# Start-up of a two-layer mixer kernel: loads in one queue in order of need, 16 KB weight rows, means from ScalarE's square, the second group's norm ahead of the output projection

## What is computed

```
h = rmsnorm(x, norm_g)                        # x * rsqrt(mean(x*x) + 1e-6) * g
a_in, a_gate, u, v, b_gate = h @ w_in         # five blocks of 512 columns
a = pool_mix(a_in) * silu(a_gate)             # trailing means over 2/4/8/16 rows, w_pool, a scale
b = u * (tril(w_s) @ rmsnorm(v, per head) + b_s) * silu(b_gate)    # chunks of 128 rows
x = x + concat(a, b) @ w_out
```

## Time and profile before

| what | value |
|---|---|
| median of three runs | 496.17 us |
| the profiled execution: its time | 495.29 us |
| its span (first to last instruction, slowest core, core 3) | 493.7 us |
| spans of the eight cores | 489.3 to 493.7 us |
| TensorE busy | 461.2 us (93%) |
| VectorE, ScalarE, GpSimd busy | 328.8, 176.2, 102.1 us |
| granted TensorE clock, core 3 | 0.987 |

### The profile page before, as it was taken

The page is one execution under the profiler, slowest core; times in us unless marked ns, Lnnn a source line. Parts: engine busy times, 40 slices in busy tenths (PEclk is TensorE's granted clock), DMA queues, the critical chain, the costliest instruction groups (busy, mean ns, idle before and its releaser), DMA issues.

```text
span 493.7 us, 7731 instructions; the slowest of 8 cores (489.3 to 493.7 us)
## 1 busy us (share of the span) xinstructions
PE 461.2 (93%) x2428; PEld 214.1 (43%) x2428; DVE 328.8 (67%) x654; ACT 176.2 (36%) x294; POOL 102.1 (21%) x142
## 2 busy tenths in 40 slices
PE   3878979999899899999999999999999999999991
PEld 1423435444444345444544445444454445444440
DVE  3666636668965768767788658655774667885665
ACT  3223251392024612229224650014800381333144
POOL 8341010510034100161015200024000500161000
PEclk9989989999999999999999999999999999999997
DMA  7999999990029500450027000000000000220013
GB/s 195 155 159 161 207 197 201 167 138 8 1 59 156 85 1 1 172 172 2 1 90 253 4 3 1 0 1 28 4 1 0 1 1 1 85 93 19 1 42 128
DMA packets 22659, 36.97 MB, mean 75 GB/s; under 512 B 1822, under 2 KB 16670, under 8 KB 22588
## 3 DMA queue, kind: packets, MB, share of 16 engines
q0 software_dynamic: 14912, 14.94, 22.1%
q1 hardware_dynamic: 6844, 20.38, 13.3%
q10 hardware_dynamic: 864, 1.16, 0.7%
...
## 4 chain that ended last, share of the span: by engine, by line
PE 83%; DMA 6%; ACT 3%; DVE 3%; issue 2%; POOL 1%; another core or an unknown queue 0%; ACTq 0%; DVEq 0%; POOLq 0%
PE pF L514 55%; PE pF L1001 19%; DMA win<-w_in 6%; PE pT L498 3%; PE pF L974 2%; PE pF L738 1%; PE pF L937 1%; ACT vscr L776 1%; POOL win L310 1%; DVE xg L1007 1%; ACT vscr L473 1%; ACT hT L811 1%; PE pF L965 1%; DVE hT L502 0%
## 5 line engine op out<-in xcount | busy, mean ns | idle before, releaser
L514 PE MATMUL pF<-hT,win 128*128 128x512 bf16 x1024 | 233.0, 381 | 4.6 <-DVE vn_sb L607 3.0
L514 PEld LDWEIGHTS pF<-hT,win 128*128 128x128 bf16 x1024 | 99.1, 98 | 121.8 <-issue 9.5
L1001 PE MATMUL pF<-wout,mix 128*128 128x512 bf16 x512 | 116.8, 383 | 2.9 <-DMA wout<-w_out 2.5
L1001 PEld LDWEIGHTS pF<-wout,mix 128*128 128x128 bf16 x512 | 49.3, 99 | 61.1 <-issue 8.0
L597 POOL TENSOR_TENSOR ss<-ss,nhalf 128x4 f32<-128x4 f32 (+1 forms) x34 | 37.2, 1094 | 152.8 <-DVE ss L595 152.6
L514 PE MATMUL pF<-win,hT 128*128 128x512 bf16 x272 | 60.8, 379 | 1.1 <-DVE hT L502 1.1
L473 ACT ACTIVATE vscr<-xg 128x1024 bf16<-128x1024 f32 x40 | 42.2, 1056 | 45.7 <-DVE xg L1007 39.0
L1007 DVE TENSOR_TENSOR xg<-pF,xg 128x512 f32<-128x512 f32 x64 | 44.0, 688 | 21.7 <-PE pF L1001 20.1
L588 ACT ACTIVATE vscr<-pF 128x512 f32<-128x512 f32 x32 | 19.1, 597 | 98.1 <-PE pF L514 68.8
L488 ACT ACTIVATE hb<-xg,ssx 128x1024 bf16<-128x1024 f32 x28 | 32.0, 1143 | 59.0 <-PE pT L498 52.3
L482 POOL TENSOR_TENSOR ssx<-ssx,nhalf 128x1 f32<-128x1 f32 (+1 forms) x22 | 15.0, 681 | 181.1 <-DVE ssx L480 163.1
...
## 6 DMA issues: line engine op xcount, KB each, us to landing
...
```

What stands on the lines that cost most here:

```text
L514: r = h.matmul(out=out_ap, lhsT=lhsT(k), rhs=rhs(k), start=(k == 0), stop=(k == 7))
L1001: r = h.matmul(out=pf[:, :], lhsT=mix[:, k, i * 128:(i + 1) * 128], rhs=wout[l][:, k, hf * 512:(hf + 1) * 512], start=(k == 0), stop=(k == 7))
```

## The change

1. The first item's loads stand in GpSimd's queue, in this order: x tiles 1 to 3, v block, v_norm_g, a_in, a_gate, w_pool, b_gate, the first part of w_s, u, first half of w_out, x tiles 4 and 5, second half of w_out, x tiles 6 and 7. SP keeps x tile 0. None of them waits for a landing any more. `prep_ws(0)` moves behind the b_gate products.
2. Layer 1's weights are issued by GpSimd in item 1, after its v tiles (`load_second`).
3. w_in, w_out and v_norm_g are laid out anew in HBM on the host. A block of 512 columns is 128 partition rows of 16 KB in one piece, where it was 1024 rows of 2 KB; v_norm_g is there 128 times instead of being read 128 times.
4. The square's `scale` is D^-0.5 (for v 128^-0.5), so its sum is the mean. The VectorE instruction for mean plus epsilon goes; epsilon is added on GpSimd, ahead of the power. The last item keeps its way, without the factor.
5. `norm_first`: tiles 2 and 3 are scaled on ScalarE.
6. Item 0: squares and scalings of the second group's tiles 0 and 1 stand ahead of `out_mm`, the others behind its first half; the first two transposes stand ahead of `out_mm(1, 1)`.

```diff
-    win_d = din("w_in", [2, D, DIN])
+    win_d = din("win_h", [2, 5, 128, 4096])
-    wout_d = din("w_out", [2, D, D])
+    wout_d = din("wout_h", [2, 2, 128, 4096])
-        win = [sb(f"win{l}", [128, 8, DIN], BF16) for l in range(2)]
+        win = [sb(f"win{l}", [128, 5, 8, 512], BF16) for l in range(2)]
...
-        for t in range(4):
-            load_tile(t)
-        for cb in WIN_ORDER:
-            if cb == C_BGATE:
-                load_wpool(0)
-            load_win(0, cb)
-        load_wout(0)
-        for cb in WIN_ORDER:
-            load_win(1, cb)
-        load_wpool(1)
+        load_tile(0)
+        for t in range(1, 4):
+            load_tile(t, eng=POOL)
         ldma(g_bc[:, 0:258], bsr_d[:, :], buf("bsf"))
-        ldma(vg_bc[:, 0, :], bc(vng_d[0:1, :]), buf("vg_bc0"), deps=[wop[f"w0_{C_V}_2"]])
-        stage(stg[:, 0:640], wsk_d[:, 0:640], [buf("mask"), buf("wsf0")], deps=[wop[f"w0_{C_AIN}_0"]])
-        for t in (4, 5):
-            load_tile(t, deps=[wop[f"w0_{C_U}_0"]])
-        for t in (6, 7):
-            load_tile(t, deps=[wop["wout0_0"]])
+        load_win(0, C_V)
+        ldma(vg_bc[:, 0, :], vng_d[0], buf("vg_bc0"), eng=POOL)
+        load_win(0, C_AIN)
+        load_win(0, C_AGATE)
+        load_wpool(0)
+        load_win(0, C_BGATE)
+        stage(stg[:, 0:640], wsk_d[:, 0:640], [buf("mask"), buf("wsf0")], eng=POOL)
+        load_win(0, C_U)
+        load_wout(0, (0,))
+        load_tile(4, eng=POOL)
+        load_tile(5, eng=POOL)
+        load_wout(0, (1,))
+        load_tile(6, eng=POOL)
+        load_tile(7, eng=POOL)
         stage(stg[:, 640:1152], wsk_d[:, 640:1152], buf("wsf1"), deps=[wop["wout0_1"]])
...
+        def rstd_from(c, cb_, rb, nparts=128):
+            pool_rsqrt(rsx[0:nparts, c:c + 1], ssx[0:nparts, c:c + 1], nhalf[0:nparts, 0:1], [cb_], [rb])
+        def pool_rsqrt(out, ms, expo, rd, wr):
+            S.emit(POOL, lambda h: h.tensor_scalar(out=out, in0=ms, scalar1=EPS, scalar2=None, op0=ALU.add), reads=rd, writes=wr)
+            S.emit(POOL, lambda h: h.tensor_tensor(out=out, in0=out, in1=expo, op=ALU.pow), reads=wr + [buf("nhalf")],
+                   writes=wr)
...
+            else:
+                S.emit(ACT, lambda h: h.activation(out=hb[:, i % NHB, :], in_=xa, func=AF.Copy, scale=rsx[:, c:c + 1]),
+                       reads=[xbuf(0, i), rb], writes=[buf(f"hb{i % NHB}")])
...
-                hk["v"] = [lambda: prep_ws(0)]
+                hk["bg"] = [lambda: prep_ws(0)]
             if n == 1:
+                hk["v"] = [load_second]
...
+        def load_second():
+            for cb in WIN_ORDER:
+                load_win(1, cb)
+            load_wpool(1)
...
             if n == 0:
+                nrm.square(0)
+                nrm.square(1)
+                nrm.rstd(0, 2)
+                nrm.scale(0)
+                nrm.scale(1)
                 for i in range(TPG):
                     out_mm(i, 0)
-                    nrm.square(i)
-                    nrm.rstd(i, 1)
-                    if i < 3:
-                        nrm.scale(i)
+                nrm.square(2)
+                nrm.rstd(2, 1)
+                nrm.scale(2)
+                nrm.square(3)
+                nrm.rstd(3, 1)
                 out_mm(0, 1)
-                out_mm(1, 1)
                 norm_tr(*nx, 0)
                 nrm.scale(3)
                 norm_tr(*nx, 1)
+                out_mm(1, 1)
                 out_mm(2, 1)
```

94 lines of the change are left out of this document (44 added, 50 removed).

## The result

The changed kernel takes **489.77 us** (median of four runs, 489.29 to 489.98) where the kernel before takes 496.10: ratio 0.987, 95% interval 0.9853 to 0.9887. In some executions of every kernel one die ran at a lower clock and the time was longer; medians here count all runs, while ratios and mean spans leave those out. The profiled execution took 489.68 us with a span of 488.1 on core 4, so the spans differ by 5.6 us from the profile before.

A forecast was written before the change was run, and what follows sets the result against it. Before 82 us, weight landings, TensorE and waits for w_out and v's scaling were taken to bound the kernel. Terms -2.1 - 2.5 - 1.8 + 0.4 + 2.1 + 0.3 = -3.6 took 496.17 to 492.6 us, range 489.8 to 496.9.

The forecast's parts named there:

- a_gate's start: Item 0: a_gate's products begin at 35.7 us instead of 37.76, worth -2.1 us; wrong if not before 37.
- the instructions called off the path: VectorE's means: 59 instructions, some 9.6 us, go without touching the critical path.
- w_out's wait, -2.5: End of item 0: w_out's second half lands at 65.3, before TensorE comes at 66.9, so its wait goes.
- the clock behind it, -1.8: Behind the w_out wait: the lowered clock goes, 16 products taking 3.46 us instead of 5.30.
- Tile 7, +0.4: End of item 0: the last x tile's late norm delays TensorE 0.4 us, between no wait and 1 us.
- Item 1, +2.1: GpSimd's six weight issues take D = 3.9 us ahead of pooling; TensorE waits D - 1.8 at the bias product, 1.7 to 3.4.
- under 1 or over 4: Sign against the forecast: item 1's wait, put at about 2 us, lies outside 1 to 4 us.
- Item 2, +0.3: Norm chains lengthened by GpSimd's addition make TensorE wait 2.0 us instead of 1.7 in item 2; 0 to 0.6.
- Part 6 at no cost: End of item 0: second-group squares and scalings lie beside the first 32 output products, 6.9 us, and cost nothing.
- the first (the loads come no faster): Before item 1: loads keep their old rate, w_out lands at 68.0, only order gains; 496.0 us, chance 0.18.
- The second, GpSimd's issues: Item 1: the six issues make the kernel slower, deciding from D = 7.5; 499.2 us at D = 10.5, chance 0.12.
- The third, the larger gain: Loads at 330 GB/s, no lowered clock at 31 us, D = 3.5, a_gate at 34.7: 490.7 to 489.2 us, chance 0.12.

The follow-up runs named there:

- e15: The changed kernel with all four first-group x scalings on VectorE, as before the change, instead of two on ScalarE: 488.64 us.
- e2: The changed kernel with w_in and w_out read in short rows of 2 KB again: 493.21 us.
- e7: The changed kernel with each of layer 1's five blocks issued in two pieces in item 1, eleven issues instead of six: 492.13 us.
- e9: The changed kernel with layer 1's weights issued at the start and the sample rows' x ahead of them in GpSimd's queue: 488.21 us.
- e3: The changed kernel with epsilon added on VectorE again, ahead of GpSimd's power, the square keeping its scale: 491.74 us.
- e8: The kernel before with long weight rows and x tiles 4 to 7 moved into GpSimd's queue: 495.9 us.
- e6: The changed kernel with the old order of squares, scalings and transposes at item 0's end: 489.61 us.
- e13: The changed kernel with epsilon on VectorE again and the old order at item 0's end, long rows kept: 495.98 us.
- e1: The kernel before with the long weight rows alone: 508.85 us.
- e5: The changed kernel with x tiles 1 to 3 back in SP's queue: 492.4 us.

## Why the prediction was right or wrong

The direction, the place of most of the gain (before 82 us) and its main mechanism were right. Three terms came out better than forecast (tile 7, item 1, item 2: 0.4, 1.35 and 1.4 us) and one worse (TensorE's arrival at w_out, 1.0), and the sum of -3.6 became -5.6 between the two profiles. The median fell by 6.4 from 496.17; the other 0.8 is no term's, as the profiled execution before lay 0.88 us under its median and the changed one only 0.09. That the time missed the range by 0.03 us and not by more or less is chance; the two steps that failed in mechanism are a_gate's start (1) and the instructions called off the path (5), and item 1 (4) is a mis-sized term.

1. **a_gate's start, -2.1: failed.** It is 37.72, where it was 37.76: the 20 products from 31.72 on take 6.0 us instead of 4.3 at the full clock. I had 34.7 without the lowered clock; it would have been 36.0, and the clock fell here in full. (On the mean of the cores it is 36.1, 36.6 before, and six of eight are under 37; in e15 it is 33.9.) I had hT of tile 3 ready at 19.4. Instead the last v products began at 20.67: x tile 1 went to a queue that brought it at 10.35 and not 9.10, and ScalarE's scaling of tile 2 held the square of tile 3. I knew of that scaling and set it against a gain of the same size that did not come; e15 shows that the scalings on ScalarE cost 1.3 us. "I am wrong if a_gate's start is not before 37" came true on the slowest core. Behind it 1.0 us came back that I had not counted: in the profile before TensorE waited 0.72 us there for a silu of ScalarE (L922), now not; it reaches w_out's second half at 61.81 + 28 x 0.216 = 67.9, 1.1 sooner than 68.93.
2. **w_out's wait, -2.5, and the clock behind it, -1.8: right.** Landing 63.72 for 65.3 forecast, no wait, full clock. 308 GB/s for the 300 that I took. My reason, that row length was not what held the old rate, was right for the most part: 1.5 of 6.3 us of earlier landing are due to it (e2, mean of the cores).
3. **Tile 7, +0.4: nothing.** Its term was at its lower bound.
4. **Item 1, +2.1: mis-sized.** D came out as 3.3, not 3.9, since an issue costs 0.55 us with 128 rows; the lower bound of 3.5 was still too high. The item became 0.75 us longer. The chain itself (issues, pooling, a_sb, ScalarE's copies, bias product) is as I gave it: e7 and e9 move the wait up and down with D. That the copies are late by 2.9 us and TensorE by only 1.1 is the 1.8 us of slack, as forecast. The sign "under 1 or over 4" did not come: 1.08, though the item as a whole grew by less than the 1.7 that I had as the least.
5. **Item 2, +0.3: wrong in sign.** It became 1.35 us shorter, by the wait at the w_pool product, 1.66 to 0.32 us (from item 2 to the end it is 1.1, as the last item grew by 0.2). Two steps failed, in about equal parts. One is "59 VectorE instructions go, off the path": VectorE set the pace of the v tiles, 2.00 us against TensorE's 1.73, and the chain that TensorE waits for in item 2 runs through them; the old means put 0.75 us back there, and 2.4 us in all (e3). The other is a term that I left at nothing: I counted the cheaper issues in item 1 only, but the two of w_out in item 2 stand in the same chain, 1.87 us before and 1.18 now, and the short rows put 0.7 us back (e2); long rows in the kernel before take the same 0.7 off (e8). GpSimd's addition, for which I took 0.2 us, costs 0.31 on average. The 0.34 that followed from the Trainium skill, "GPSIMD Engine Reference", section 3, is the nearer one, and it mattered as little as the prediction said.
6. **Part 6 at no cost: right, and at no gain** (e6), but only because part 4 does the same work (e13).

Of the rivals, the first (the loads come no faster) is out: 308 GB/s for 288, and even with short rows (e2) w_out came at 66.37, 1.6 sooner than that rival had it. The rule cited there, that row length is worth nothing from 512 bytes on, comes out nearly so for the transfers: up to w_out's landing 307 GB/s with long rows and 300 with short ones, in the mean of the cores (e2). The 3.3 us that the rows are worth lie nearly all in GpSimd's issues, of which the rule says nothing. The second, GpSimd's issues, would decide from D = 7.5; D was 3.3, and e7 supports the price of a us per us. Beside item 1's v tiles an issue took 0.56 us, and w_out's two at the start 0.54, so a lengthening by VectorE hardly shows. The third, the larger gain, named 490.7 for D = 3.5 and an early a_gate: the time is near, the way is another one, as a_gate was not early. The rival that I did not see is that the long rows make the kernel slower when x tiles that are needed soon stand in SP's queue: by 13 us with tiles 4 to 7 there (e1 against e8), by 2.6 with tiles 1 to 3 (e5). The change put those tiles into GpSimd's queue, and nothing in the trace before, where no row was long, told that this part of it was what made the other possible.

What stays open: what about 1 us of the old means' price before item 1 consists of, why e13's times spread more than the others', how far the 68 GB/s depend on the row length (only 2 KB and 16 KB were tried), and what v_norm_g's new layout is worth, which no run undoes alone.
